# Decoder trunk on one core: the opening fed by half weight pieces for both token tiles, x loaded in quarters and split out of PSUM

## What is computed

```python
x = x + HALF_STEP * swiglu(rmsnorm(x, norm_ffn1[l]), w1_gate[l], w1_up[l], w1_down[l])

def swiglu(x, w_gate, w_up, w_down):
    return (jax.nn.silu(x @ w_gate) * (x @ w_up)) @ w_down
```

## Time and profile before

| what | value |
|---|---|
| median of three runs | 962.52 us |
| the profiled execution, its own time | 963.35 us |
| its span, first to last instruction | 961.3 us |
| TensorE matmul busy | 947.7 us (99%) |
| TensorE weight load busy | 783.7 us (82%) |
| VectorE busy | 555.1 us (58%) |
| ScalarE busy | 458.8 us (48%) |
| GpSimd busy | 206.9 us (22%) |
| mean granted TensorE clock | 0.998 |

### The profile page before, as it was taken

One profiled execution on the slowest core, in us unless ns is written; L12 is line 12 of the kernel. 1 busy time (PEld: TensorE's weight loads), 2 busy tenths in 40 slices (PEclk: granted clock), 3 DMA queues, 4 the chain that ended last, 5 costly groups with the idle time before them and its releaser, 6 DMA issues.

```text
span 961.3 us, 12595 instructions
## 1 busy us (share of the span) xinstructions
PE 947.7 (99%) x4379; PEld 783.7 (82%) x4379; DVE 555.1 (58%) x623; ACT 458.8 (48%) x580; POOL 206.9 (22%) x237
## 2 busy tenths in 40 slices
PE   8999999999999999999999999999999999999997
PEld 6788888888888888888888888888888888888885
DVE  5554555666575555554666555556665755555554
ACT  7443444455564444444445444444556445444442
POOL 4343521000010332121023113210001024313210
PEclk9999999999999999999999999999999999999999
DMA  8789676735354887675747767574624647867651
GB/s 277 204 211 232 212 240 196 246 123 169 117 174 133 219 228 231 192 226 195 249 118 212 252 191 230 185 224 152 226 82 175 218 117 203 272 187 227 187 163 44
DMA packets 166051, 185.98 MB, mean 193 GB/s; under 512 B 49264, under 2 KB 139424, under 8 KB 166016
## 3 DMA queue, kind: packets, MB, share of 16 engines
q1 hardware_dynamic: 122080, 174.09, 55.4%
q10 hardware_dynamic: 43616, 10.52, 6.5%
q0 software_dynamic: 320, 0.92, 0.7%
HBM read 173.96 MB, written 1.05 MB: 182 GB/s over the span
## 4 chain that ended last, share of the span: by engine, by line
PE 91%; DMA 3%; ACT 2%; DVE 2%; POOL 1%; issue 1%; SPq 1%; ACTq 0%; POOLq 0%; DVEq 0%
PE gu L871 19%; PE gu L873 19%; PE gu L872 19%; PE acc L873 10%; PE acc L871 10%; PE acc L872 10%; DMA kT<-kT 2%; ACT w_hi L360 1%; DMA raw<-in_w_up_dram 1%; PE tp L1007 1%; DVE w_lo L596 1%; PE tp L889 1%; PE acc L1018 1%; PE tp L1030 1%; ACT rT L397 0%
## 5 line engine op out<-in xcount | busy, mean ns | idle before, releaser
L596 DVE TENSOR_TENSOR w_lo<-raw,w_hi 128x2048 fp32r<-128x2048 f32 (+1 forms) x164 | 372.8, 2277 | 153.5 <-ACT w_hi L360 153.4
L871 PE MATMUL gu<-w_hi,xT_hi 128*128 128x512 f32 x892 | 350.1, 393 | 2.6 <-DVE w_lo L596 1.6
L873 PE MATMUL gu<-w_hi,xT_lo 128*128 128x512 f32 x892 | 347.4, 389 | 0.0
L872 PE MATMUL gu<-w_lo,xT_hi 128*128 128x512 f32 x892 | 347.2, 389 | 0.0
L360 ACT ACTIVATE w_hi<-raw 128x2048 fp32r<-128x2048 f32 (+1 forms) x164 | 305.5, 1866 | 14.5 <-DMA raw<-in_w_in_dram 7.2
L871 PEld LDWEIGHTS gu<-w_hi,xT_hi 128*128 128x128 f32 x892 | 167.5, 188 | 39.5 <-DVE w_lo L596 3.3
L873 PEld LDWEIGHTS gu<-w_hi,xT_lo 128*128 128x128 f32 x892 | 167.4, 188 | 35.0
L872 PEld LDWEIGHTS gu<-w_lo,xT_hi 128*128 128x128 f32 x892 | 167.5, 188 | 33.7
L871 PE MATMUL acc<-w_hi,aT_hi 128*128 128x512 f32 x384 | 150.7, 392 | 0.1
L873 PE MATMUL acc<-w_hi,aT_lo 128*128 128x512 f32 x384 | 149.7, 390 | 0.0
L872 PE MATMUL acc<-w_lo,aT_hi 128*128 128x512 f32 x384 | 149.5, 389 | 0.0
(11 more groups left out here) (129 smaller groups left out, 433.6 us busy)
## 6 DMA issues: line engine op xcount, KB each, us to landing
raw<-in_w_down_dram SPq DMA_DIRECT2D x88, 512.0 KB, 4.1
raw<-in_w_gate_dram SPq DMA_DIRECT2D x84, 512.0 KB, 4.0
raw<-in_w_up_dram SPq DMA_DIRECT2D x84, 512.0 KB, 5.0
raw<-in_w_in_dram SPq DMA_DIRECT2D x40, 512.0 KB, 4.7
raw<-in_w_out_dram SPq DMA_DIRECT2D x16, 512.0 KB, 4.1
raw<-in_w_in_dram SPq DMA_DIRECT2D x16, 256.0 KB, 2.9
raw<-in_w_gate_dram SPq DMA_DIRECT2D x8, 256.0 KB, 4.0
raw<-in_w_up_dram SPq DMA_DIRECT2D x8, 256.0 KB, 5.5
```

What stands on the lines that cost most here:

```text
L596: nc.vector.tensor_tensor(w_lo[:, pos % SLOTS, 0:n], raw[:, pos % RAW, 0:n], w_hi[:, pos % SLOTS, 0:n].bitcast(F32), ALU.subtract).then_in ...
L871: nc.tensor.matmul(out_, s_hi, m_hi, start=first, stop=False)
L872: nc.tensor.matmul(out_, s_hi, m_lo, start=False, stop=False)
L873: return nc.tensor.matmul(out_, s_lo, m_hi, start=False, stop=last)
```

## The change

In the opening x is loaded in quarters (one tile, one half of the columns each): the first half of tile 0 ahead of the weights, the first half of tile 1 behind the first half of piece 0, the two second halves behind the second half of piece 0. The semaphore `x_half_loaded[tt]` counts the first half of a tile, `x_loaded[tt]` now counts the second. The four blocks of a quarter are transposed into banks `tp[0]`, `acc[0]`, `tp[1]`, `acc[1]`. The high part of the first quarter is made by VectorE straight from PSUM in one instruction; of the other three by ScalarE in four 128x128 instructions each, scaled by the gains; all low parts by VectorE in four 128x128 instructions each, from PSUM. `wide` is not written. TensorE uses each half piece for tile 0 and then for tile 1 (`first_slices`). Step 1 of this FFN writes `acc[2]` and `acc[3]` in place of the `gu` banks and no longer waits for `hidden_done`; the down products of step 0 wait for it instead, tile 0 for two, tile 1 for four. ScalarE takes both sums of squares behind the split of piece 2. Cut to its core:

```diff
+            def load_x(tt, half):
+                cols = slice(half * 512, (half + 1) * 512)
+                sp.dma_start(x[:, tt, cols], x_in[0, tt * P:(tt + 1) * P, cols]).then_inc((x_half_loaded, x_loaded)[half][tt], 16)
-            sp.dma_start(x[:, 0, :], x_in[0, 0:P, :]).then_inc(x_loaded[0], 16)
+            load_x(0, 0)
...
                                 sp.dma_start(dst[:, :, g, :], w[layer, rows, 0:CH].rearrange("(k p) n -> p k n", p=P)).then_inc(loaded[pos], 16)
+                            if (layer, pos, part) == (0, 0, 0):
+                                load_x(1, 0)
+                            if (layer, pos, part) == (0, 0, 1):
+                                load_x(0, 1)
+                                load_x(1, 1)
...
-                if (layer, base) == (0, 0):
-                    sp.dma_start(x[:, 1, :], x_in[0, P:2 * P, :]).then_inc(x_loaded[1], 16)
...
+            def first_x_hi(tt, half, bank):
+                act.wait_ge(gT_done, 1)
+                act.wait_ge(xT_psum, tt + 2 * half + 1)
+                for k in range(4):
+                    kt = 4 * half + k
+                    ins = nc.scalar.activation(xT_hi[:, kt, tt * P:(tt + 1) * P], bank[:, k * P:(k + 1) * P], ACT.Copy, scale=gT[:, kt:kt + 1])
+                ins.then_inc(xT_hi_done, 1)
+
+            act.sem_inc(xT_hi_done, 1)
             first_half_hi(0, 0)
-            xT_half(0, 0, 1)
+            first_x_hi(1, 0, acc[0])
             second_half_hi(0, 0)
-            split_first_hi(0, 1)
-            squares(0, 0)
-            xT_parts(0, 1)
+            first_x_hi(0, 1, tp[1])
+            first_half_hi(0, 1)
+            first_x_hi(1, 1, acc[1])
+            second_half_hi(0, 1)
             split_hi(0, 2)
-            squares(0, 1)
+            for tt in range(TT):
+                act.wait_ge(x_half_loaded[tt], 16)
+                squares(0, tt)
...
             dve.wait_ge(x_loaded[0], 16)
             dve.sem_inc(x_new, 2)
             dve.wait_ge(gT_done, 1)
-            xT_parts(0, 0, 0)
-            split_first_lo(0, 1)
+            dve.wait_ge(xT_psum, 1)
+            nc.vector.tensor_tensor(xT_hi[:, 0:4, 0:P], tp[0][:, :].rearrange("p (k n) -> p k n", k=4),
+                                    gT[:, 0:4].unsqueeze(2).broadcast_to([P, 4, P]), ALU.mult).then_inc(x_first_hi, 1)
+
+            def first_x_lo(tt, half, bank, when, count):
+                dve.wait_ge(when, count)
+                for k in range(4):
+                    kt, ts = 4 * half + k, slice(tt * P, (tt + 1) * P)
+                    ins = nc.vector.scalar_tensor_tensor(xT_lo[:, kt, ts], bank[:, k * P:(k + 1) * P], gT[:, kt:kt + 1],
+                                                         xT_hi[:, kt, ts].bitcast(F32), ALU.mult, ALU.subtract)
+                ins.then_inc(xT_lo_done, 1)
+
+            first_x_lo(0, 0, tp[0], x_first_hi, 1)
+            split_first_lo(0, 0, [0])
             dve.wait_ge(x_loaded[1], 16)
             dve.sem_inc(x_new, 2)
-            xT_parts(0, 1, 0)
+            dve.sem_inc(xg_done, 4)
+            first_x_lo(1, 0, acc[0], xT_hi_done, 2)
+            split_first_lo(0, 0, [1])
+            first_x_lo(0, 1, tp[1], xT_hi_done, 3)
+            split_first_lo(0, 1, [0])
+            first_x_lo(1, 1, acc[1], xT_hi_done, 4)
+            split_first_lo(0, 1, [1])
...
+            def first_slices(h, part, tt, hook=None):
+                ts = slice(tt * P, (tt + 1) * P)
+                kts = range(4 * h + 2 * part, 4 * h + 2 * part + 2)
...
+                go(xT_hi, w_hi, (h, part) == (0, 0))
+                pe.wait_ge(xT_lo_done, 2 * h + tt + 1)
+                go(xT_lo, w_hi)
+                if hook:
+                    hook()
+                if tt == 0:
+                    if part == 0:
+                        pe.wait_ge(lo_half, h + 1)
+                    else:
+                        pe.wait_ge(lo_done, h + 1 + RAW)
+                return go(xT_hi, w_lo, last=(h, part) == (1, 1))
...
+                def first_up():
+                    for h in range(2):
+                        for part in range(2):
+                            for tt in range(TT):
+                                ins = first_slices(h, part, tt, {(0, 0, 0): lambda: first_x_T(1, 0, acc[0]), (0, 1, 0): second_x_halves}.get((h, part, tt)))
...
-                for tt in range(TT):
+                if i == 0:
+                    first_up()
+                    up(e0 + 2, 0, 2, 0, guard=False, bank=acc[2])
+                    up(e0 + 3, 0, 2, 1, guard=False, bank=acc[3])
...
+                for tt in range(TT):
+                    if i == 0:
+                        pe.wait_ge(hidden_done, 2 * tt + 2)
                     down((dT_lo_done, d0 + tt + 1), 0, 4, 0, tt, first=True)
...
-            enter_T(0, 0)
-            warm(18)
+            first_x_T(0, 0, tp[0])
+            warm(16)
```

More of the change, by code:

```diff
@@ L128, in build @@
         x_loaded = [sem(f"x_loaded{i}") for i in range(TT)]
+        x_half_loaded = [sem(f"x_half_loaded{i}") for i in range(TT)]
         gains_loaded, gT_psum, gT_done = sem("gains_loaded"), sem("gT_psum"), sem("gT_done")
@@ L415, in ffn, with silu @@
                 s0, d0 = STEPS * i, 2 * (STEPS - 1) * i
-                def silu(s_, tt, it, pos):
+                def silu(s_, tt, it, pos, banks=gu):
                     if tt == 0:
@@ L422, in silu @@
                         act.wait_ge(slot_free, SLOTS + LP * layer + SLOTS * it + base + pos + 1)
-                    nc.scalar.activation(silu_g[:, tt, :], gu[tt][:, 0:CH], ACT.Silu, scale=rstd[:, tt:tt + 1]).then_inc(silu_done, 1)
+                    nc.scalar.activation(silu_g[:, tt, :], banks[tt][:, 0:CH], ACT.Silu, scale=rstd[:, tt:tt + 1]).then_inc(silu_done, 1)
                 def turn(d, tt):
@@ L476, in ffn @@
                 step(s0, d0, 0, 0, 1, pieces(0, 3, 4, None))
-                step(s0 + 1, d0 + 2, 1, 0, 3, pieces(0, 5, 6, 7))
+                step(s0 + 1, d0 + 2, 1, 0, 3, pieces(0, 5, 6, 7), gu if i else acc[2:4])
                 with act.Fori(0, LOOPED) as it:
@@ L660, in ffn, with hide @@
                 e0, d0 = 2 * STEPS * i, 2 * (STEPS - 1) * i
-                def hide(e, tt, guard=None):
+                def hide(e, tt, guard=None, banks=gu):
                     dve.wait_ge(silu_done, e + 1)
@@ L712, in ffn @@
                 step(e0, d0, 0, 0, pieces(0, 3, 4, None), False)
-                step(e0 + 2, d0 + 2, 1, 0, pieces(0, 5, 6, 7))
+                step(e0 + 2, d0 + 2, 1, 0, pieces(0, 5, 6, 7), True, gu if i else acc[2:4])
                 with dve.Fori(0, LOOPED) as it:
@@ L890, in enter_T, with go, project @@
                     ins.then_inc(xT_psum, 1)
-            def project(layer, it, tt, pos, n_pieces, ready, hook=None, entry=None, halved=False):
+            def first_slices(h, part, tt, hook=None):
+                ts = slice(tt * P, (tt + 1) * P)
+                kts = range(4 * h + 2 * part, 4 * h + 2 * part + 2)
+                def go(x_, w, first=False, last=False):
+                    for kt in kts:
+                        ins = nc.tensor.matmul(gu[tt][:, :], x_[:, kt, ts], w[:, h, kt % 4 * 512:(kt % 4 + 1) * 512],
+                                               start=first and kt == kts[0], stop=last and kt == kts[1])
+                    return ins
+                if tt == 0:
+                    if part == 0:
+                        pe.wait_ge(hi_half, h + 1)
+                    else:
+                        pe.wait_ge(hi_done, h + 1)
+                if (h, tt) == (0, 0):
+                    pe.wait_ge(x_first_hi, 1)
+                else:
+                    pe.wait_ge(xT_hi_done, 2 * h + tt + 1)
+                go(xT_hi, w_hi, (h, part) == (0, 0))
[3 more added lines that the diff above has]
+                    hook()
+                if tt == 0:
+                    if part == 0:
+                        pe.wait_ge(lo_half, h + 1)
+                    else:
+                        pe.wait_ge(lo_done, h + 1 + RAW)
+                return go(xT_hi, w_lo, last=(h, part) == (1, 1))
+            def project(layer, it, tt, pos, n_pieces, ready, hook=None, entry=None, halved=False, bank=None):
                 kk = KT // n_pieces
@@ L1126, in _, with first_x_T @@
             nc.tensor.transpose(gu[0][:, 0:n], gain_rows, ident[0:n, 0:n]).then_inc(gT_psum, 1)
-            enter_T(0, 0)
-            warm(18)
+            def first_x_T(tt, half, bank):
+                pe.wait_ge((x_half_loaded, x_loaded)[half][tt], 16)
+                for k in range(4):
+                    c = (4 * half + k) * P
+                    ins = nc.tensor.transpose(bank[:, k * P:(k + 1) * P], x[:, tt, c:c + P], ident[:, :])
+                ins.then_inc(xT_psum, 1)
+            first_x_T(0, 0, tp[0])
+            warm(16)
             for layer in range(DEPTH):
```

41 lines of the change are left out of this document (23 added, 18 removed).

## The result

The changed kernel took 971.42 us as the median of six runs (969.44 to 972.73), the kernel before 962.15 in its six. The ratio is 1.0088 with a 95% interval of 1.0074 to 1.0102: slower by 0.9%, 9.3 us between the medians, where 7.7 us were forecast (970.2). The profiled execution took 972.73, its span is 970.8 us.

What follows compares the result with a forecast made beforehand. TensorE was taken to bound the kernel, so opening losses reach the end: 5.1 us from the opening plus 2.55 from the new wait, about 7.7 on 962.5, gave 970.2 us, range 965.8 to 974.2.

Steps and rivals of the forecast that it cites:

- The kept wait: Opening: VectorE's unchanged wait on x_loaded[0] now counts tile 0's second half, so VectorE starts at 10.45, not 6.24.
- The serial chain: Opening, from VectorE's first x instruction through TensorE and ScalarE's row: silu of step 0 at 27.0 instead of 21.89, +5.1 us.
- the rival with 0.27: TensorE's clock falls at one of the opening's new idle gaps: 972.1 us, or 974 for two falls; chance 0.27.
- The new wait: Step 0's second down product waits for hide of step 1, tile 1: TensorE idles 3.9 us to 46.6, net 2.55.
- its cheap rival: Step 0, tile 1's transposing DMA takes half of 7.50 us, hide comes 3.75 earlier: 966.8 us; chance 0.10.
- Banks apart worth nothing: Step 1 in acc[2], acc[3]: dropping its hidden_done wait gains nothing, as 22.9 was just in time for 23.2.
- No new waits after 55: Behind the opening: TensorE meets no new waits after 55 us.
- a granted clock under 1.00 before 55: Sign in the changed profile's opening that would mean the clock's case.
- the clock's case: Opening: idle gaps bring TensorE's half clock, 1.85 us per fall: 972.1 us with one, 974 with two; chance 0.27.
- the plain forecast: Whole kernel with no certain clock fall: 970.2 us, 5.1 from the opening and 2.55 from the wait; chance 0.45.
- not slower: Opening: ScalarE's row is short enough, silu of step 0 by 19.5, about 962.7 us; deciding point 19.3; chance 0.10.

Runs made afterwards that it cites:

- f1_wait_moved: a0_plain with VectorE's waits for both second halves of x moved behind its second group of small instructions: 965.59 us, ratio 1.0033 to the kernel before.
- a0_plain: Changed kernel with each transposing DMA of the FFNs' hidden block replaced by two plain copies (the changed plain base): 968.13 us, ratio 1.0069 to the kernel before.
- b1_banks: b0_plain with only the change's banks and their waits on hidden_done, old opening kept: 963.55 us, ratio 1.0008 to the kernel before.
- g0_gu_banks: a0_plain with step 1 back in the gu banks under the old guards, no hidden_done waits at step 0's down products: 967.86 us, ratio 1.0058.
- g3_reordered: f1_wait_moved plus g0_gu_banks, VectorE making all quarters' high parts, squares ahead of piece 2's split, second halves transposed earlier, 8 identity transposes for 16: 961.22 us.
- b0_plain: Kernel before with each transposing DMA of the FFNs' hidden block replaced by two plain copies (the plain base): 961.44 us, ratio 0.9992 to the kernel before.
- f4_warm: a0_plain with 32 identity transposes instead of 16 ahead of the first matmul and 20 more between pieces 2 and 3: 968.40 us, ratio 1.0059.
- h1_table_early: g3_reordered plus one single-column silu on ScalarE behind piece 2's split, to load the table early: 959.39 us, ratio 0.9974 to the kernel before.

## Why the prediction was right

**The kept wait: right.** VectorE's start was put at 10.45 by interpolating landings; it was 10.16, the first matmul 11.00 for 11.2. f1_wait_moved shows the cause and its price, 2.5 to 3.5 us.

**The serial chain: right, and 2.1 us too short.** `silu` was put 5.1 us later and came 7.2 later. Three terms were mis-sized. ScalarE's four small instructions, taken as 0.85 with 1.02 called an upper bound, took 1.14: the bound came from a similar form and was none. Three groups, which overlap their neighbours a little, make 0.7 us. The clock fell at the first gap, the rival with 0.27, and stood in the chain: from the start of the two low matmuls at 12.07 to ScalarE's group at 14.24 are 2.2 us, where 0.46 and 0.6 were taken, 1.1 us more. (In a0_plain, at full clock until 32.8, the whole chain is 0.9 shorter.) And GpSimd's powers were not beside the table load: the first instruction took 1.26 us, from 26.24 until VectorE's split of piece 2 was over, and the fourth ended at 29.06, 0.6 behind the end of the load, where 0.1 was taken. That is 0.5. TensorE's row ahead of the third quarter took 0.2 more than put, and the earlier landing gave 0.3 back: 2.2 in sum for the 2.1.

**The new wait: right in mechanism, too large.** `hide` of step 1, tile 1 was put at 46.6 and ended at 46.25, out of two errors: everything 2.1 later, and the transposing DMA of the earlier trace rows 5.01 us instead of 7.50. The forecast had this as its cheap rival with half the landing. So TensorE waited 1.34 us and not 3.9, since it was itself later. At piece 5 the two errors cancel: forecast 49.4, measured 49.17. That the point was met so closely is luck. On the plain base the cause stands alone in b1_banks, 1.5 us. On the late opening it is worth 1.7 us at piece 5 and 1.3 to 1.8 us between executions at full clock; in the medians it can't be told from nothing.

**Banks apart worth nothing: right.** g0_gu_banks takes them back and loses nothing; the freed banks only move an idle stretch.

**No new waits after 55: wrong.** The profiled execution has 0.7 us in two waits at 520 and 524, behind a landing of 7.15 us, and 1.1 us at 805, behind the landing of 8.37 us. The forecast treated everything behind the opening as a pure shift. The kernel before stands as close to these waits: its own landing there was 7.37 us. In the two plain bases the shift is pure. But g3_reordered, whose mixer starts at 189.99 as in b0_plain, takes 183.5 us from its transposes at 478 to those at 662 where b0_plain takes 182.4, behind a copy that landed in 5.88 us, and f4_warm takes 183.3 behind one of 6.33. (The changed kernel takes 183.7 there, the kernel before 182.4.) So a late landing costs about 1 us in that stretch without any shift of the opening, and with plain copies too. That the changed kernel's 2 us are the same thing is likely from this; for the wait at 805 it is not shown.

**The sum.** The forecast's 7.7 and the bases' 7.4 agree, with the opening 2.1 too short and the new wait 2.5 too long: the agreement of the sums is partly luck. By the prediction's own sign, a granted clock under 1.00 before 55, the profiled execution is the clock's case (972.1) and not the plain forecast. The six executions say something like it: the one with a mean granted clock of 0.999 took 969.44, the two with 0.995 took 972.12 and 972.26, the three with 0.997 from 969.46 to 972.73. So what the median has over the forecast lies in the clock and in the later waits, in shares that one profile doesn't give. The margins of ScalarE's row and the clock were inside the range of 965.8 to 974.2. The rival "not slower" was judged right: its point was `silu` at 19.3, and only h1_table_early, with all the edits above together, came near (19.95). The Trainium skill, TensorE: Matmul & The Clock Gate, section "HAM oscillation — how this bites in real kernels", has the price paid anew at each gap. The traces agree only in part. Gaps stood ahead of the falls in the changed kernel (2.80 us) and in a0_plain (3.23 us), but gaps as long cost no clock elsewhere: 3.23 us ahead of piece 3 in the changed kernel, 3.24 in f1_wait_moved; and b1_banks fell with no gap over 1.01 us from its first product on. Beside f4_warm, a0_plain's fall cost nothing, because a wait stood behind it.

## What to carry to other kernels

When a transfer is cut into parts and its semaphores are renamed, read every wait on the old name, those that the diff leaves alone most of all: one of them here cost 2.5 to 3.5 us. A bank taken to spare one wait makes another where it is next written; look up when its last reader runs, and what stands ahead of that reader on its engine. And an early start is worth what the last wait of the stretch lets through: here that was the first `silu`, so what counts is the row of instructions ahead of it, down to a table load that stands behind a wait.

## What the runs showed of the hardware

- Four ScalarE copies of 128x128 from PSUM with a scale for each partition took 1.14 us, one ScalarE copy of 128x512 from SBUF without a scale 0.63, one VectorE multiply of 128x512 from PSUM 0.69 us; the accumulating squares from which the bound came started 0.25 us apart with their reads. The four small ones are dearer here than the same columns in one; how much of it is their number, the scale or PSUM, no run separates.
- The table load went behind one of `silu`'s two waits and not behind the other. In g3_reordered it began at 19.95, after 2.31 us of idleness in which it could have run, when the product was there. In the changed kernel, where the product was the earlier one, it ran from 27.21, while `silu` still waited for GpSimd's power until 29.06.
- The clock's falls differ from execution to execution and aren't bound to the change: at 12.0 in the changed kernel's profile, at 32.8 in a0_plain, at 13.4 in b1_banks with the old opening, where TensorE had been working with short gaps before.
- GpSimd's multiply-add on a single column took 1.26 us beside VectorE's split of piece 2 and 0.19 us, at 28.24, without it. It ended 0.05 to 0.06 us behind the end of VectorE's instruction each time: 27.50 after 27.44 in the changed kernel, 23.54 after 23.49 in f1_wait_moved, 21.22 after 21.17 in the kernel before.
